# Prompt mixers: VectorE puts the level masks on the product as it leaves PSUM

## The chip, the cores and the metric

One core of one Trainium2 chip runs the whole step in one launch. The time is device microseconds of that core, the median of several executions. The profile is one execution, recorded by the hardware profiler; its times are counted from the start of its span.

## What is computed

One layer of a hybrid decoder over 2048 prompt tokens and 64 sample tokens: an input projection, three kinds of recurrent mixers (mLSTM, gated DeltaNet, HGRN2), an output projection and a squared-ReLU feed-forward. The change lies in the gated-DeltaNet part of the prompt mixers. For each of 6 heads and each chunk of tokens it needs the solution of a unit lower triangular system:

```python
lmat = where(strict, einsum('bhtk,bhsk->bhts', kb, kh) * exp(where(strict, diff, 0.0)), 0.0)
rhs = concatenate([vh * bh[..., None], kb * exp(g)[..., None]], axis=-1)
sol = triangular_solve(eye + lmat, rhs, left_side=True, lower=True, unit_diagonal=True)
```

## The kernel before

The stages run one after another: prologue, input projection, gates, prompt mixers, sample mixers, output projection, feed-forward. The prompt mixers (`prompt_mixers`) take 16 tiles of 128 tokens. Within each tile, all 6 heads are handled side by side in tiles of 128 x 6 x 128 elements (768 columns).

The inverse of identity plus L is built up by halving, in `LEVELS` = 7 levels. Level 0 handles pairs, level 1 groups of four, and so on. `lt` is the transposed matrix L (L2295, from PSUM `pa` and the decays `bd`). `x` is the inverse so far and `xt` its transpose; at each level only the off-diagonal corners of the level's blocks are new. A level is a ring over the engines:

- TensorE, `level_product(l)` (L1948): the level's part of -L times `x`, into `pa` or `pb`.
- ScalarE, `copy(l)` (L2060): that product from PSUM into `m1`.
- TensorE, `level_update(l)` (L1963): first `onto`, which puts `x` into PSUM through an identity matrix, then six products with `m1` on top of it (released by `m1_copy`), then six products of `m1` with `xt`, the change of the transpose.
- ScalarE, `inverse(l)` (L2070): the new `x` from PSUM. VectorE, `update(l)` (L2271): adds the change to `xt` (L2282).

In levels 0 to 4 (below `BLOCKY` = 5) the level's part of L is a masked and negated copy `cl[l % 3]`, which GpSimd makes (L2182), five products of 768 columns per tile, from `lt` and the mask `level`. Levels 5 and 6 use one negated copy `ltr` of the whole of `lt`, made by ScalarE (L2093) for every tile already, and take only the corners out of PSUM (L2067, L2277, L2287).

The order of the work is written out by hand, engine by engine, and engines meet through counted semaphores. The groups between the levels are the rest of the tile before: on TensorE `state_queries`, `mlstm`, `solved`, `hgrn`, `outputs`, `states`, `finish`. On VectorE they are the normalisation of the mLSTM (`den`, L2311 to L2313), the next tile's decays (L2238 `mix_cc`, L2240 `mix_dc`, L2243 `mix_ex`) between levels 1 and 2, `y`, `hs` and `hq` (L2321 to L2336) between 2 and 3, and `gs`, `cm` and the sum of squares `ss` (L2343 to L2351) between 3 and 4. On GpSimd the `cl` products are followed by `hk` (L2188, L2190), which waits for `e` and for TensorE's `hgrn` group (semaphore `ho`), then, after VectorE's `hq`, by the differences of the next tile (L2164, L2159) and its `bd` (L2149, L2151). VectorE's scaling of `y` by the head norms is L2359.

Of the kernel before, what the change touches and what calls it, by code (L numbers as in the profile page):

```python
# [8 lines left out]
F32 = mybir.dt.float32  # L9
F32R = mybir.dt.float32r  # L10
ALU = mybir.AluOpType
ACT = mybir.ActivationFunctionType
AX = mybir.AxisListType

P = 128
# [7 lines left out]
MH, GH, HH = 6, 6, 4  # L23
# [833 lines left out]
LEVELS = P.bit_length() - 1  # L857
HEADS_BY_PAIR = [0, 3, 1, 4, 2, 5]
BLOCKY = 5
# [818 lines left out]
def prompt_mixers(nc, d, keep):  # L1678

    with ExitStack() as ctx:  # L1680
# [8 lines left out]
        late = sb("late", [P, 2, P])  # L1689
        bd = sb("bd", [P, MH, P])  # L1690
        pm, at_, lt, xf, wn = (sb(n, [P, MH, P]) for n in ("pm", "attn", "lt", "xf", "wn"))
        cl = sb("cl", [P, 3, MH, P], F32R)
        x, xt, m1 = (sb(n, [P, MH + 1, P], F32R) for n in ("x", "xt", "m1"))
        ltr = sb("ltr", [P, MH, P], F32R)
        blocky = {l: sb(f"m1_{l}", [P, MH + 1, P], F32R) for l in range(BLOCKY, LEVELS)}
# [18 lines left out]
        pa, pb, pc, pd = bank("pa"), bank("pb"), bank("pc"), bank("pd")  # L1714
        za_in, zb_in, zg_in, rb_in, y_out = ([S(f"{n}{u}") for u in range(2)] for n in ("za_in", "zb_in", "zg_in", "rb_in", "y_out"))
        picked = [S(f"picked{par}") for par in range(2)]
        CONSTS = 2
        const_n = 64
        W = HD + 1
        U = 2 * (LEVELS - 1)  # L1720
# [96 lines left out]
        @block.tensor  # L1817
        def _(pe):
            pe.wait_ge(S("const_in"), const_n)
            pe.wait_ge(S("consts"), CONSTS)  # L1820

            def body(t, u, r, first=False, last=False, tail=False):
# [123 lines left out]
                    mm.then_inc(S("round"), 1)  # L1946

                def level_product(l):  # L1948
                    if l < BLOCKY:
                        pe.wait_ge(S("cl"), v(BLOCKY, l + 1))  # L1950
                    else:
                        pe.wait_ge(S("ltr"), v(1, 1))
                    lhs = lambda h: cl[:, l % 3, h, :] if l < BLOCKY else ltr[:, h, :]
                    if l:
                        pe.wait_ge(S("x"), v(LEVELS, l))
                        six(product_in(l), lhs, lambda h: pair_of(x, h), "m1")
                        return
                    if not first:
                        pe.wait_ge(S("xf"), b(1, 1))
                    onto(pb, ident_r[:, 0, :], lambda par: ident_r[:])  # L1960
                    add(pb, lhs, lambda h: ident_r[:, 2:4, :], "m1")
# [73 lines left out]
        def _(act):  # L2035
# [20 lines left out]
            def body(t, u, r, first=False, last=False, tail=False):  # L2056
                v = lambda n, c: t * n + c
                b = lambda n, c: t * n + c - n

                def copy(l):  # L2060
                    act.wait_ge(S("m1"), v(LEVELS, l + 1))
                    src = pv(product_in(l), P)
                    if l < BLOCKY:
                        act.activation(hm(m1[:, 0:MH]), src, ACT.Copy).then_inc(S("m1_copy"), 1)
                        return
                    for rows, cols in corners(l):
                        ins = act.activation(hm(m1_of(l)[rows, 0:MH, cols]), src[rows, :, :, cols], ACT.Copy)  # L2067
                    ins.then_inc(S("m1_copy"), 1)
# [70 lines left out]
        @block.gpsimd  # L2139
        def _(pool):  # L2140
            pool.memset(zero[:], 0.0).then_inc(S("zero"), 1)
            pool.wait_ge(S("zero"), 1)
            pool.wait_ge(S("const_in"), const_n)
            pool.wait_ge(S("consts"), CONSTS)

            def decays(t, u):

                pool.wait_ge(S("ex"), t + 1)
                pool.tensor_tensor(bd[:], ex[u][:, :, 1, :], rb[u][:, :, 2, :], ALU.mult).then_inc(S("bd"), 1)  # L2149
                pool.wait_ge(S("bd"), t * 2 + 1)  # L2150
                pool.tensor_tensor(bd[:], bd[:], late[:, 1:2, :].broadcast_to([P, MH, P]), ALU.mult).then_inc(S("bd"), 1)  # L2151

            def differences(t, u, r):

                g = zb[u][:, B_HG0:NBR:2, :]
                pool.wait_ge(zb_in[u], 32 * (r + 1))
                for l in range(LEVELS + 2):
                    if l == LEVELS:
                        ins = pool.tensor_tensor(e[:, l], g, zero[:].unsqueeze(2).broadcast_to([P, 2, P]), ALU.add)  # L2159
                        continue  # L2160
                    size, at = (2 << l, (1 << l) - 1) if l < LEVELS else (P, P - 1)
                    gv = g.rearrange("p j (n b) -> p j n b", b=size)
                    for j in range(2):
                        ins = pool.tensor_tensor(e[:, l, j].rearrange("p (n b) -> p n b", b=size), gv[:, j],  # L2164
                                                 gv[:, j, :, at:at + 1].broadcast_to([P, P // size, size]), ALU.subtract)
                ins.then_inc(S("diff"), 1)

            differences(0, 0, 0)
            decays(0, 0)

            def body(t, u, r, first=False, last=False, tail=False):
                v = lambda n, c: t * n + c
                b = lambda n, c: t * n + c - n
                if tail:
                    return
                pool.wait_ge(S("lt"), v(1, 1))
                for l in range(BLOCKY):
                    if l >= 3:
                        pool.wait_ge(S("m1"), v(LEVELS, l - 2))
                    if l == 3:  # L2180
                        pool.wait_ge(S("xt"), v(LEVELS, 1))
                    pool.tensor_tensor(cl[:, l % 3], lt[:], level[:, l + 1:l + 2, :].broadcast_to([P, MH, P]), ALU.mult  # L2182
                                       ).then_inc(S("cl"), 1)
                kr = zb[u][:, B_HG0 + 1:NBR:2, :]
                pool.wait_ge(S("e"), v(1, 1))
                if not first:
                    pool.wait_ge(S("ho"), b(1, 1))
                pool.tensor_tensor(hk[:, 0:LEVELS], e[:, 0:LEVELS], kr.unsqueeze(1).broadcast_to([P, LEVELS, 2, P]),  # L2188
                                   ALU.mult).then_inc(S("hk"), 1)
                pool.tensor_tensor(hk[:, LEVELS], e[:, LEVELS + 1], kr, ALU.mult).then_inc(S("hk"), 1)  # L2190
                if not last:
                    pool.wait_ge(S("hq"), v(1, 1))
                    pool.wait_ge(S("hk"), v(2, 2))
                    differences(t + 1, 1 - u, r + u)
                    decays(t + 1, 1 - u)
            tiles(body)

        @block.vector
        def _(dve):
# [15 lines left out]
                dve.memset(tile[:].bitcast(F32), 0.0)  # L2215
            dve.tensor_scalar(ident_r[:, 3, :], keep["ident"][:], 0.0, None, ALU.mult)
            dve.tensor_scalar(ident_2[:], keep["ident"][:], 2.0, None, ALU.mult)
            dve.tensor_copy(ident_r[:, 0:3, :], keep["ident"][:].unsqueeze(1).broadcast_to([P, 3, P])).then_inc(S("level_read"), 1)
            dve.wait_ge(S("level_read"), 1)
            dve.tensor_scalar(level[:], level[:], -1.0, None, ALU.mult).then_inc(S("consts"), 1)  # L2220
            ident4 = keep["ident"][:].unsqueeze(1).unsqueeze(1).broadcast_to([P, 2, 3, P])
            dve.wait_ge(S("consts"), CONSTS)
            STEPS = 32
# [24 lines left out]
            def body(t, u, r, first=False, last=False, tail=False):  # L2248
# [20 lines left out]
                                ins.then_inc(S("masked"), 1)  # L2269

                def update(l):  # L2271
                    if l >= BLOCKY:
                        dve.wait_ge(S("u"), v(U, 2 * l - 1))
                        dve.wait_ge(S("x"), v(LEVELS, l))
# [29 lines left out]
                    then(dve.tensor_tensor(hm(num[:]), pv(pd, W, 3 * W), colh(o, Q_WI, W), ALU.mult))  # L2304
                    dve.tensor_tensor(hm(num[:]), hm(num[:]), pv(pd, W), ALU.add).then_inc(S("num"), 1)
                if not tail:
                    dve.wait_ge(S("cl"), v(BLOCKY, 1))
                    dve.tensor_tensor(hm(xt[:, 0:MH]), ident4, hm(cl[:, 0].bitcast(F32)), ALU.add).then_inc(S("xt"), 1)
                if not first:
                    dve.wait_ge(S("num"), b(1, 1))  # L2310
                    then(dve.scalar_tensor_tensor(den[:, 0, :], num[:, :, HD], -1.0, num[:, :, HD], ALU.mult, ALU.max))  # L2311
# [756 lines left out]
```

## Time and profile before

| | us |
|---|---|
| median of 3 runs | 3625.7 (3625.65 to 3627.26) |
| profiled execution, its own time | 3626.71 |
| its span | 3624.9 |

| engine | busy us | share of the span |
|---|---|---|
| TensorE | 3286.9 | 91% |
| VectorE | 1829.1 | 50% |
| ScalarE | 1414.2 | 39% |
| GpSimd | 430.5 | 12% |

Shares over the whole span mix stages with different limits: GpSimd works in the mixers alone. The prompt mixers lie between about 980 and 1720 us. A timeline gives an instruction's start and duration on its engine; an entry with xN covers N instructions of one line. What stands in brackets is the idle time of the engine before it and what ended it. Durations of consecutive instructions overlap slightly. In the page the granted clock of TensorE over the span is 0.951 of full.

### The profile page before, as it was taken

What the parts mean: (1) busy time and instruction counts of PE and PEld (TensorE: products, weight loads), DVE (VectorE), ACT (ScalarE), POOL (GpSimd) and SP (SyncE); (2) the same over time, 40 slices, a digit from 0 to 9 for tenths busy, and PEclk for the clock granted to TensorE, in tenths of its full rate; (3) what the DMA queues carried; (4) which work ended last, traced back from release to release, by engine and by line L of the source; (5) the groups of instructions that cost most, each with busy time, mean ns of one, the idle gap of its engine ahead of it and who ended that gap; (6) DMA issues with size and microseconds to landing.
All of it is one profiled execution on the core that took longest, in us unless ns stands there. A gap on an engine that the chain in (4) does not pass through costs nothing. (4 is left out here: it accounts for less than half of the span.)

```text
span 3624.9 us, 52375 instructions
## 1 busy us (share of the span) xinstructions
PE 3286.9 (91%) x21605; PEld 2986.4 (82%) x21605; DVE 1829.1 (50%) x2931; ACT 1414.2 (39%) x2100; POOL 430.5 (12%) x442
## 2 busy tenths in 40 slices
PE   4899999998289899898569889999999999999998
PEld 3799999998278888787548679999999999999987
DVE  6232333221278888886457634454454454454465
ACT  6333422322145455553035433343343343333454
POOL 0000000000166565552200000000000000000000
PEclk6999999999599999998679989999999999999999
DMA  5222323221722222221246473344354344343353
GB/s 195 50 60 66 72 72 83 84 68 54 263 77 88 88 94 96 88 76 39 76 142 219 182 254 133 127 175 150 118 191 151 127 164 152 133 160 142 134 206 115
DMA packets 232385, 449.98 MB, mean 124 GB/s; under 512 B 41382, under 2 KB 115292, under 8 KB 228028
## 3 DMA queue, kind: packets, MB, share of 16 engines
q1 hardware_dynamic: 230020, 428.07, 34.9%
q10 hardware_dynamic: 2128, 18.56, 1.4%
q8 instruction: 172, 2.82, 0.3%
q14 instruction: 65, 0.53, 0.0%
HBM read 363.11 MB, written 83.47 MB: 123 GB/s over the span
## 5 line engine op out<-in xcount | busy, mean ns | idle before, releaser
L2779 PE MATMUL ff_p<-ff_h_hi,ff_w_hi 128*128 128x384 f32 (+1 forms) x1536 | 502.9, 327 | 24.9 <-DMA ff_h_lo<-tmp_h 24.9
L2781 PE MATMUL ff_p<-ff_h_hi,ff_w_lo 128*128 128x384 f32 (+1 forms) x1536 | 503.1, 328 | 0.0
L2780 PE MATMUL ff_p<-ff_h_lo,ff_w_hi 128*128 128x384 f32 (+1 forms) x1536 | 502.3, 327 | 0.0
L412 PE MATMUL pin_pz<-hi,pin_whi 128*128 128x424 f32 (+1 forms) x1320 | 469.0, 355 | 14.2 <-DVE pin_wlo L528 14.2
L413 PE MATMUL pin_pz<-lo,pin_whi 128*128 128x424 f32 (+1 forms) x1320 | 466.7, 354 | 0.0
L414 PE MATMUL pin_pz<-hi,pin_wlo 128*128 128x424 f32 (+1 forms) x1320 | 466.6, 353 | 0.0
L2798 PE MATMUL ff_p<-ff_w_lo,ff_f_hi 128*128 128x512 f32 (+1 forms) x1088 | 426.7, 392 | 0.0
L2799 PE MATMUL ff_p<-ff_w_hi,ff_f_lo 128*128 128x512 f32 (+1 forms) x1088 | 426.5, 392 | 0.0
L2797 PE MATMUL ff_p<-ff_w_hi,ff_f_hi 128*128 128x512 f32 (+1 forms) x1088 | 423.8, 389 | 0.0
L2882 DVE TENSOR_TENSOR ff_w_lo<-ff_w,ff_w_hi 128x1024 fp32r<-128x1024 f32 x192 | 235.1, 1224 | 346.4 <-ACT ff_w_hi L2830 346.4
L2830 ACT ACTIVATE ff_w_hi<-ff_w 128x1024 fp32r<-128x1024 f32 x192 | 203.6, 1060 | 389.0 <-PE ff_p L2799 384.6
L2779 PEld LDWEIGHTS ff_p<-ff_h_hi,ff_w_hi 128*128 128x128 f32 x1536 | 290.2, 189 | 34.0 <-DMA ff_h_lo<-tmp_h 25.0
L447 ACT ACTIVATE pin_z<-pin_pz,cols 128x424 f32<-128x424 f32 (+1 forms) x165 | 114.4, 702 | 515.5 <-PE pin_pz L414 416.8
L2780 PEld LDWEIGHTS ff_p<-ff_h_lo,ff_w_hi 128*128 128x128 f32 x1536 | 290.1, 189 | 7.3
L2838 ACT ACTIVATE ff_relu<-ff_p 128x384 f32<-128x384 f32 (+1 forms) x192 | 90.9, 473 | 515.4 <-PE ff_p L2781 515.4
L2781 PEld LDWEIGHTS ff_p<-ff_h_hi,ff_w_lo 128*128 128x128 f32 x1536 | 290.0, 189 | 0.0
L2890 DVE TENSOR_TENSOR ff_sq<-ff_relu 128x384 f32<-128x384 f32 (+1 forms) x192 | 102.7, 535 | 364.5 <-ACT ff_relu L2838 364.5
L528 DVE TENSOR_TENSOR pin_wlo<-pin_w,pin_whi 128x1024 fp32r<-128x1024 f32 x33 | 40.4, 1225 | 479.4 <-ACT pin_whi L440 479.4
L2877 DVE TENSOR_TENSOR ff_w_lo<-ff_w,ff_w_hi 128x1024 fp32r<-128x1024 f32 x192 | 235.0, 1224 | 83.0 <-ACT ff_w_hi L2823 66.2
L412 PEld LDWEIGHTS pin_pz<-hi,pin_whi 128*128 128x128 f32 x1320 | 248.6, 188 | 19.4 <-issue 15.3
L413 PEld LDWEIGHTS pin_pz<-lo,pin_whi 128*128 128x128 f32 x1320 | 248.8, 188 | 5.1 <-issue 1.0
L414 PEld LDWEIGHTS pin_pz<-hi,pin_wlo 128*128 128x128 f32 x1320 | 248.8, 188 | 4.2
(522 smaller groups left out, 5526.2 us busy)
## 6 DMA issues: line engine op xcount, KB each, us to landing
ff_w<-in_w_unit SPq DMA_DIRECT2D x192, 512.0 KB, 5.2
ff_w<-in_w_unit SPq DMA_DIRECT2D x48, 2048.0 KB, 8.0
tmp_z<-pin_z SPq DMA_DIRECT2D x32, 1024.0 KB, 5.2
mix_rb<-tmp_rows_p SPq DMA_DIRECT2D x16, 1152.0 KB, 5.7
pin_w<-in_w_in SPq DMA_DIRECT2D x33, 512.0 KB, 5.0
gat_wa<-in_w_ada ACTq DMA_DIRECT2D x8, 2048.0 KB, 28.3
mix_zb<-tmp_z SPq DMA_DIRECT2D x16, 640.0 KB, 4.2
tmp_h<-op_h_hi SPq DMA_DIRECT2D x17, 512.0 KB
```

The lines of the kernel that those rows point to most:

```text
L412: pe.matmul(pz[:, g, 0:n], whi[:, u, k], hi[:, k, at:at + n], start=(k == 0), stop=False)
L413: pe.matmul(pz[:, g, 0:n], whi[:, u, k], lo[:, k, at:at + n], start=False, stop=False)
L414: mm = pe.matmul(pz[:, g, 0:n], wlo[:, u, k], hi[:, k, at:at + n], start=False, stop=(k == KT - 1))
L2779: pe.matmul(dst, w1_hi[:, u, k], hi, start=(k == 0), stop=False)
L2780: pe.matmul(dst, w1_hi[:, u, k], lo, start=False, stop=False)
L2781: mm = pe.matmul(dst, w1_lo[:, u, k], hi, start=False, stop=(k == KT - 1))
L2797: pe.matmul(dst, f_hi[:, u, cols], w2_hi[:, u, ocs, :], start=(j == 0), stop=False)
L2798: pe.matmul(dst, f_hi[:, u, cols], w2_lo[:, u, ocs, :], start=False, stop=False)
L2799: mm = pe.matmul(dst, f_lo[:, u, cols], w2_hi[:, u, ocs, :], start=False, stop=(j == J - 1))
L2830: act.activation(w2_hi[:, c % 2], w2[:, four % 2, :, c % 4, :], ACT.Copy).then_inc(w2_hi_ready, 1)
L2877: dve.tensor_tensor(w1_lo[:, c % 2], w1[:, c % 4], w1_hi[:, c % 2].bitcast(F32), ALU.subtract).then_inc(w1_lo_ready, 1)
L2882: dve.tensor_tensor(w2_lo[:, c % 2], w2[:, (c // 4) % 2, :, c % 4, :], w2_hi[:, c % 2].bitcast(F32), ALU.subtract).then_inc(w2_lo_ready, 1)
```

## The change

The level masks move from the operand to the result. GpSimd makes one `cl`, for level 0, from the negated mask `level_n`. Levels 1 to 4 multiply with `ltr`, the whole negated matrix, and VectorE multiplies the product by the level's mask as it takes it out of PSUM into `m1` (in `update(l)`, ahead of its wait for TensorE's second group). The masks for this stand transposed in `level_t`; TensorE transposes them once at the start and VectorE copies them from PSUM. ScalarE's copies of levels 1 to 4 go, and `level` is no longer negated as a whole.

```diff
@@ -1689,7 +1689,9 @@
         late = sb("late", [P, 2, P])
         bd = sb("bd", [P, MH, P])
         pm, at_, lt, xf, wn = (sb(n, [P, MH, P]) for n in ("pm", "attn", "lt", "xf", "wn"))
-        cl = sb("cl", [P, 3, MH, P], F32R)
+        cl = sb("cl", [P, MH, P], F32R)
+        level_n = sb("level_n", [P, P])
+        level_t = sb("level_t", [P, BLOCKY - 1, P])
         x, xt, m1 = (sb(n, [P, MH + 1, P], F32R) for n in ("x", "xt", "m1"))
         ltr = sb("ltr", [P, MH, P], F32R)
         blocky = {l: sb(f"m1_{l}", [P, MH + 1, P], F32R) for l in range(BLOCKY, LEVELS)}
@@ -1714,7 +1716,7 @@
         pa, pb, pc, pd = bank("pa"), bank("pb"), bank("pc"), bank("pd")
         za_in, zb_in, zg_in, rb_in, y_out = ([S(f"{n}{u}") for u in range(2)] for n in ("za_in", "zb_in", "zg_in", "rb_in", "y_out"))
         picked = [S(f"picked{par}") for par in range(2)]
-        CONSTS = 2
+        CONSTS = 3
         const_n = 64
         W = HD + 1
         U = 2 * (LEVELS - 1)
@@ -1817,6 +1819,9 @@
         @block.tensor
         def _(pe):
             pe.wait_ge(S("const_in"), const_n)
+            for l in range(1, BLOCKY):
+                mm = pe.transpose(pa[:, 0, (l - 1) * P:l * P], level[:, l + 1, :], keep["ident"][:])
+            mm.then_inc(S("masks"), 1)
             pe.wait_ge(S("consts"), CONSTS)
 
             def body(t, u, r, first=False, last=False, tail=False):
@@ -1946,11 +1951,11 @@
                     mm.then_inc(S("round"), 1)
 
                 def level_product(l):
-                    if l < BLOCKY:
-                        pe.wait_ge(S("cl"), v(BLOCKY, l + 1))
+                    if l == 0:
+                        pe.wait_ge(S("cl"), v(1, 1))
                     else:
                         pe.wait_ge(S("ltr"), v(1, 1))
-                    lhs = lambda h: cl[:, l % 3, h, :] if l < BLOCKY else ltr[:, h, :]
+                    lhs = lambda h: ltr[:, h, :] if l else cl[:, h, :]
                     if l:
                         pe.wait_ge(S("x"), v(LEVELS, l))
                         six(product_in(l), lhs, lambda h: pair_of(x, h), "m1")
@@ -2058,11 +2063,10 @@
                 b = lambda n, c: t * n + c - n
 
                 def copy(l):
+                    if l < BLOCKY:
+                        return
                     act.wait_ge(S("m1"), v(LEVELS, l + 1))
                     src = pv(product_in(l), P)
-                    if l < BLOCKY:
-                        act.activation(hm(m1[:, 0:MH]), src, ACT.Copy).then_inc(S("m1_copy"), 1)
-                        return
                     for rows, cols in corners(l):
                         ins = act.activation(hm(m1_of(l)[rows, 0:MH, cols]), src[rows, :, :, cols], ACT.Copy)
                     ins.then_inc(S("m1_copy"), 1)
@@ -2174,13 +2178,7 @@
                 if tail:
                     return
                 pool.wait_ge(S("lt"), v(1, 1))
-                for l in range(BLOCKY):
-                    if l >= 3:
-                        pool.wait_ge(S("m1"), v(LEVELS, l - 2))
-                    if l == 3:
-                        pool.wait_ge(S("xt"), v(LEVELS, 1))
-                    pool.tensor_tensor(cl[:, l % 3], lt[:], level[:, l + 1:l + 2, :].broadcast_to([P, MH, P]), ALU.mult
-                                       ).then_inc(S("cl"), 1)
+                pool.tensor_tensor(cl[:], lt[:], level_n[:].unsqueeze(1).broadcast_to([P, MH, P]), ALU.mult).then_inc(S("cl"), 1)
                 kr = zb[u][:, B_HG0 + 1:NBR:2, :]
                 pool.wait_ge(S("e"), v(1, 1))
                 if not first:
@@ -2215,9 +2213,10 @@
                 dve.memset(tile[:].bitcast(F32), 0.0)
             dve.tensor_scalar(ident_r[:, 3, :], keep["ident"][:], 0.0, None, ALU.mult)
             dve.tensor_scalar(ident_2[:], keep["ident"][:], 2.0, None, ALU.mult)
-            dve.tensor_copy(ident_r[:, 0:3, :], keep["ident"][:].unsqueeze(1).broadcast_to([P, 3, P])).then_inc(S("level_read"), 1)
-            dve.wait_ge(S("level_read"), 1)
-            dve.tensor_scalar(level[:], level[:], -1.0, None, ALU.mult).then_inc(S("consts"), 1)
+            dve.wait_ge(S("masks"), 1)
+            dve.tensor_copy(level_t[:], pa[:, 0, :].rearrange("p (l c) -> p l c", c=P)).then_inc(S("consts"), 1)
+            dve.tensor_scalar(level_n[:], level[:, 1, :], -1.0, None, ALU.mult)
+            dve.tensor_copy(ident_r[:, 0:3, :], keep["ident"][:].unsqueeze(1).broadcast_to([P, 3, P])).then_inc(S("consts"), 1)
             ident4 = keep["ident"][:].unsqueeze(1).unsqueeze(1).broadcast_to([P, 2, 3, P])
             dve.wait_ge(S("consts"), CONSTS)
             STEPS = 32
@@ -2269,6 +2268,10 @@
                                 ins.then_inc(S("masked"), 1)
 
                 def update(l):
+                    if l < BLOCKY:
+                        dve.wait_ge(S("m1"), v(LEVELS, l + 1))
+                        dve.tensor_tensor(hm(m1[:, 0:MH]), pv(product_in(l), P), level_t[:, l - 1, :].unsqueeze(1).unsqueeze(1)
+                                          .broadcast_to([P, 2, 3, P]), ALU.mult).then_inc(S("m1_copy"), 1)
                     if l >= BLOCKY:
                         dve.wait_ge(S("u"), v(U, 2 * l - 1))
                         dve.wait_ge(S("x"), v(LEVELS, l))
@@ -2304,8 +2307,8 @@
                     then(dve.tensor_tensor(hm(num[:]), pv(pd, W, 3 * W), colh(o, Q_WI, W), ALU.mult))
                     dve.tensor_tensor(hm(num[:]), hm(num[:]), pv(pd, W), ALU.add).then_inc(S("num"), 1)
                 if not tail:
-                    dve.wait_ge(S("cl"), v(BLOCKY, 1))
-                    dve.tensor_tensor(hm(xt[:, 0:MH]), ident4, hm(cl[:, 0].bitcast(F32)), ALU.add).then_inc(S("xt"), 1)
+                    dve.wait_ge(S("cl"), v(1, 1))
+                    dve.tensor_tensor(hm(xt[:, 0:MH]), ident4, hm(cl[:].bitcast(F32)), ALU.add).then_inc(S("xt"), 1)
                 if not first:
                     dve.wait_ge(S("num"), b(1, 1))
                     then(dve.scalar_tensor_tensor(den[:, 0, :], num[:, :, HD], -1.0, num[:, :, HD], ALU.mult, ALU.max))
```

The VectorE queue of a tile in the middle, around levels 1 and 2. `mix_m` is `m1`; `mix_pa` and `mix_pb` are PSUM. Before:

```order
L2313 RECIPROCAL mix_den<-mix_den 128x6
L2282 TENSOR_TENSOR mix_xt<-mix_xt,mix_pa 128x768
L2238 TENSOR_SCALAR mix_cc<-cols_p 128x48
L2240 TENSOR_SCALAR mix_dc<-mix_dec 64x6 x2
L2243 TENSOR_TENSOR mix_ex<-mix_rb,mix_late 128x1536
L2282 TENSOR_TENSOR mix_xt<-mix_xt,mix_pb 128x768
```

And now:

```order
L2316 RECIPROCAL mix_den<-mix_den 128x6
L2273 TENSOR_TENSOR mix_m<-mix_pa,mix_level_t 128x768
L2285 TENSOR_TENSOR mix_xt<-mix_xt,mix_pa 128x768
L2237 TENSOR_SCALAR mix_cc<-cols_p 128x48
L2239 TENSOR_SCALAR mix_dc<-mix_dec 64x6 x2
L2242 TENSOR_TENSOR mix_ex<-mix_rb,mix_late 128x1536
L2273 TENSOR_TENSOR mix_m<-mix_pb,mix_level_t 128x768
L2285 TENSOR_TENSOR mix_xt<-mix_xt,mix_pb 128x768
```

The mask products of levels 1 and 2 stand ahead of the `xt` of their level; the second stands behind the three lines of the decays.

The same queue around levels 3 and 4. Before:

```order
L2336 TENSOR_TENSOR mix_hq<-mix_e,mix_zb 128x2048
L2282 TENSOR_TENSOR mix_xt<-mix_xt,mix_pa 128x768
L2343 SCALAR_TENSOR_TENSOR mix_gs<-mix_gs,mix_dc,mix_pc 128x64 x3
L2347 SCALAR_TENSOR_TENSOR mix_cm<-mix_cm,mix_dc,mix_pc 128x65 x3
L2351 TENSOR_REDUCE mix_ss<-mix_sq 128x16
L2282 TENSOR_TENSOR mix_xt<-mix_xt,mix_pb 128x768
```

And now:

```order
L2339 TENSOR_TENSOR mix_hq<-mix_e,mix_zb 128x2048
L2273 TENSOR_TENSOR mix_m<-mix_pa,mix_level_t 128x768
L2285 TENSOR_TENSOR mix_xt<-mix_xt,mix_pa 128x768
L2346 SCALAR_TENSOR_TENSOR mix_gs<-mix_gs,mix_dc,mix_pc 128x64 x3
L2350 SCALAR_TENSOR_TENSOR mix_cm<-mix_cm,mix_dc,mix_pc 128x65 x3
L2354 TENSOR_REDUCE mix_ss<-mix_sq 128x16
L2273 TENSOR_TENSOR mix_m<-mix_pb,mix_level_t 128x768
L2285 TENSOR_TENSOR mix_xt<-mix_xt,mix_pb 128x768
```

The masks of levels 3 and 4 stand behind `hq` and behind the sum `ss`.

The ScalarE queue around level 1 (`vn` from the `solved` group, then `kd`). Before:

```order
L2089 ACTIVATE mix_vn<-mix_pc 128x384
L2064 ACTIVATE mix_m<-mix_pa 128x768
L2093 ACTIVATE mix_ltr<-mix_lt 128x768
L2096 ACTIVATE mix_y<-mix_pd 128x2x2x64
L2097 ACTIVATE mix_kd<-mix_pd 128x256
L2072 ACTIVATE mix_x<-mix_pb 128x768
L2064 ACTIVATE mix_m<-mix_pb 128x768
L2072 ACTIVATE mix_x<-mix_pa 128x768
```

And now:

```order
L2093 ACTIVATE mix_vn<-mix_pc 128x384
L2097 ACTIVATE mix_ltr<-mix_lt 128x768
L2100 ACTIVATE mix_y<-mix_pd 128x2x2x64
L2101 ACTIVATE mix_kd<-mix_pd 128x256
L2076 ACTIVATE mix_x<-mix_pb 128x768
L2076 ACTIVATE mix_x<-mix_pa 128x768
```

The copies to `m1` are gone, and `ltr` directly follows `vn`.

## Rows read from the trace of the kernel before

**Rows 1.** Stretches: busy us (instructions) per engine, granted clock, DMA share, GB/s.

```profile
1432.60:1476.00 43.40, 39.71 (x458) 35.53 (x454) 36.23 (x79) 22.92 (x41) 25.34 (x26) 1.00 0.27 92
...
1476.00:1523.30 47.30, 41.20 (x456) 36.76 (x454) 39.20 (x78) 22.92 (x41) 25.23 (x26) 0.96 0.25 84
```

**Rows 2.** Timeline, VectorE: start us, duration us, engine, line; `mix_lt` of five tiles.

```profile
1210.56 0.95 DVE L2295 TENSOR_TENSOR mix_lt<-mix_pa,mix_bd 128x768 f32<-128x768 f32 x1
...
1259.13 0.95 DVE L2295 TENSOR_TENSOR mix_lt<-mix_pa,mix_bd 128x768 f32<-128x768 f32 x1
...
1432.61 0.95 DVE L2295 TENSOR_TENSOR mix_lt<-mix_pa,mix_bd 128x768 f32<-128x768 f32 x1
...
1475.97 0.95 DVE L2295 TENSOR_TENSOR mix_lt<-mix_pa,mix_bd 128x768 f32<-128x768 f32 x1
...
1523.31 0.95 DVE L2295 TENSOR_TENSOR mix_lt<-mix_pa,mix_bd 128x768 f32<-128x768 f32 x1
```

**Rows 3.** Timeline, VectorE and TensorE: scaling of `y` in two tiles, TensorE's wait.

```profile
1459.58 1.34 DVE L2359 TENSOR_TENSOR mix_y<-mix_y,mix_ss 128x1024 f32<-128x1024 f32 x1
...
1502.93 4.42 DVE L2359 TENSOR_TENSOR mix_y<-mix_y,mix_ss 128x1024 f32<-128x1024 f32 x1
...
1508.25 0.95 PE L1841 MATMUL mix_pb<-mix_x,mix_ltr 128*128 128x256 f32 x6 [2.61 <-DVE mix_x L2277]
```

**Rows 4.** Timeline of the steady tile, level 1; [idle before <-releaser] in brackets.

```profile
1433.64 9.71 POOL L2182 TENSOR_TENSOR mix_cl<-mix_lt,mix_level 128x768 fp32r<-128x768 f32 x5 [11.25 <-DVE mix_lt L2295]
...
1437.14 0.79 ACT L2072 ACTIVATE mix_x<-mix_pb 128x768 fp32r<-128x768 f32 x1
...
1438.08 0.95 PE L1841 MATMUL mix_pa<-mix_x,mix_cl 128*128 128x256 f32 x6
...
1438.69 0.49 ACT L2089 ACTIVATE mix_vn<-mix_pc 128x384 f32<-128x384 f32 x1
...
1439.08 0.81 ACT L2064 ACTIVATE mix_m<-mix_pa 128x768 fp32r<-128x768 f32 x1
...
1439.90 0.84 ACT L2093 ACTIVATE mix_ltr<-mix_lt 128x768 fp32r<-128x768 f32 x1
...
1440.89 0.70 PE L1923 MATMUL mix_pb<-mix_x,mix_ident_r 128*128 128x512 f32 x2
...
1443.11 0.95 DVE L2282 TENSOR_TENSOR mix_xt<-mix_xt,mix_pa 128x768 fp32r<-128x768 f32 x1 [1.31 <-PE mix_pa L1841]
```

**Rows 5.** Timeline of the steady tile, level 2.

```profile
1443.32 4.01 POOL L2188 TENSOR_TENSOR mix_hk<-mix_e,mix_zb 128x1792 f32<-128x1792 f32 x1
...
1443.98 3.40 DVE L2238 TENSOR_SCALAR mix_cc<-cols_p 128x48 f32<-128x48 f32 x1
...
1446.42 0.86 PE L1929 MATMUL mix_pa<-mix_m,mix_xt 128*128 128x256 f32 x6
...
1447.13 0.87 PE L1841 MATMUL mix_pb<-mix_xt,mix_m 128*128 128x256 f32 x6
...
1448.27 1.76 DVE L2243 TENSOR_TENSOR mix_ex<-mix_rb,mix_late 128x1536 f32<-128x1536 f32 x1
...
1449.94 0.95 DVE L2282 TENSOR_TENSOR mix_xt<-mix_xt,mix_pb 128x768 fp32r<-128x768 f32 x1
```

**Rows 6.** Timeline of the steady tile, levels 3 and 4.

```profile
1451.51 0.97 PE L1929 MATMUL mix_pb<-mix_m,mix_xt 128*128 128x256 f32 x6
...
1452.32 0.88 PE L1841 MATMUL mix_pa<-mix_xt,mix_m 128*128 128x256 f32 x6
...
1452.38 2.28 DVE L2336 TENSOR_TENSOR mix_hq<-mix_e,mix_zb 128x2048 f32<-128x2048 f32 x1
...
1454.59 0.94 DVE L2282 TENSOR_TENSOR mix_xt<-mix_xt,mix_pa 128x768 fp32r<-128x768 f32 x1
...
1456.16 0.87 PE L1929 MATMUL mix_pa<-mix_m,mix_xt 128*128 128x256 f32 x6
...
1457.78 0.95 DVE L2282 TENSOR_TENSOR mix_xt<-mix_xt,mix_pb 128x768 fp32r<-128x768 f32 x1
```

## The prediction

> **What bounds the kernel now.** I read the page first: TensorE is busy 91% of the span, and the change touches only the prompt mixers, where 16 tiles of 128 tokens pass one after another. Then the stretches by engine: a steady tile keeps TensorE busy 39.7 of 43.4 us at the full granted clock, VectorE 36.2, ScalarE 22.9, GpSimd 25.3 [rows 1]. So TensorE bounds the tile, VectorE is second, ScalarE has half its time free. What the change takes away (ScalarE, GpSimd) was spare; what it adds goes to the engine with least room beside TensorE.
>
> Third, the length of a tile, from one `mix_lt` to the next: 1432.61 to 1475.97 is 43.36 us. Two of the 16 are longer: the one from 1210.56 to 1259.13 (48.57) and the one from 1475.97 to 1523.31 (47.34) [rows 2]. In the second the row-wise scaling of `y` (L2359) took 4.42 us instead of 1.34, and TensorE waited 2.61 us behind it for `x` [rows 3]; in the first it is the same picture. Together they cost 5.20 + 3.97 = 9.2 us over the steady tile. The `y` instruction accounts for 3.1 us of each; the other 2.1 and 0.9 are TensorE at half speed (1.2 of 2.4 GHz) after its wait: the granted clock of the second is 0.96, that of the steady tile 1.00 [rows 1].
>
> Last, the timeline of the steady tile, level by level. Each level is a ring: product (TensorE), copy of the product to `m1`, update (TensorE), copy of `x` (ScalarE), next product. TensorE fills the copy's time with a group of the tile before, so the copy of 0.8 us is hidden.
>
> **The change part by part.** I write times on the clock of the steady tile and let the delay D grow.
>
> Level 1, the negated matrix `ltr`. Product 1 used `cl`, there since long, and started 0.15 us after `x` (1437.14 + 0.79 = 1437.93) at 1438.08. Now it needs `ltr`, whose copy stands on ScalarE behind the near copies and `vn`. The `m1` copy ahead of it goes, so `ltr` starts where that one did, 1439.08, and ends 0.84 later at 1439.92; product 1 follows at 1440.07. **D = 1.99** [rows 4]. The mask itself (0.95 us, as `mix_lt`, also a product of PSUM and an SBUF matrix [rows 2], against 0.81 for ScalarE's copy [rows 4]) ends near 1442.0. TensorE's own fill, from product 1 to the update, is 2.81 us (1438.08 to 1440.89) and ends later, at 1442.88. So the mask costs nothing here; without that fill it would cost 1.1.
>
> Level 2. VectorE's order now is: `xt` of level 1, then the next tile's decays (L2238, L2240, L2243), then mask 2. ScalarE had copied `m1` with nothing ahead of it. The decays end at a time that GpSimd sets: `mix_cc`, a copy of 48 columns, took 3.40 us because it sat until the first `hk` (1443.32 + 4.01 = 1447.33) was done [rows 5]. Does `hk` now start earlier, with four of the five `cl` products gone (9.71 us for five [rows 4], 1.9 each)? No: it also waits for TensorE's group behind product 1, which ended near 1441.1 and now ends D later, at 1443.1. So `hk` stays where it was, `mix_ex` still ends near 1449.94, and mask 2 runs 1449.94 to 1450.89. The update's masked half starts 0.14 later at 1451.03, where before it was at 1446.42: **D = 4.61** [rows 5].
>
> The Trainium skill (SBUF — State Buffer, Who interferes with whom) says that a VectorE instruction with two SBUF inputs, or in a two-port mode, is fully blocked by a GpSimd instruction that holds the shared port. The 3.40 us of `mix_cc` agree. By it, fewer GpSimd products are a gain for VectorE's small instructions ahead of level 1; by the rows it is none, since VectorE then waits 1.31 us for TensorE before `xt` [rows 4]. If the port alone set the end there, the sum would be 15 x 1.3 = 20 us lower than mine.
>
> Level 3. `xt` of level 2 waited for the decays before (1449.94) and now waits for TensorE's second half, 1447.13 + 0.87 + 4.61 = 1452.61, so it starts at 1452.72. From there to the end of `hq` is 4.72 us as before (1454.66 less 1449.94), since the same instructions stand between. `hq` ends at 1457.44, mask 3 runs 1457.37 to 1458.32 (consecutive instructions overlap by 0.07, as 1454.59 shows), the update gets its matrix at 1458.46 against 1451.51: **D = 6.95** [rows 6].
>
> Level 4. `xt` of level 3 now waits for TensorE, 1452.32 + 0.88 + 6.95 = 1460.15, start 1460.25. The state updates and the sum `ss` stand behind it; from there to the next level's instruction it was 3.19 us (1454.59 to 1457.78). Mask 4 runs 1463.44 to 1464.39, the update gets it at 1464.53 against 1456.16: **D = 8.37** [rows 6]. Levels 5 and 6 are untouched, and behind them TensorE and VectorE are near full, so nothing is made up.
>
> Sum: 15 tiles x 8.37 = +125.6. The first tile has none of the fills on VectorE except decays and `hq`; I take +4, an estimate of half a tile's loss, with 0 and 8.4 as ends. The constants (four transposes, a 512-column copy for a scaling of 1024 columns) come to +0.3, an estimate, ends -1 and +2. The collision of `y` should go: `hq` ends at 1457.44, GpSimd's differences after it took some 7 us before, so they end near 1464.5, while `y` moves by D to 1467.95 [rows 3, 6]. That returns the 9.2 us; ends 0 and -9.2. Subtotal **+120.7**.
>
> **The clock.** New waits of TensorE per tile, each the time above less my estimate of the end of the fill before it: about 1.8 us before product 1, 2.5 at level 2, 2.9 at level 3, 1.8 at level 4. The two waits of 2.6 us in the trace were each followed by half clock, worth 2.13 and 0.9 us, mean 1.5. With two waits per tile of that size, not each of which need bring the fall, I take 1.4 falls per tile: 2.1 x 15 = **+31.5**. Below, the bound is 0; above, TensorE stays at half clock through the levels: a group of six products of 256 columns takes 0.95 at full clock, about 0.7 more at half, and eight such groups stand in the ring from product 1 to update 4: 5.6 per tile, +84.
>
> Total +152 on the profiled span of 3624.9, that is 3777. The profiled run itself took 3626.7, the median is 3625.7, so the forecast is **3778**.
>
> The Trainium skill (VectorE: DVE Perf Modes, Specifications) says that VectorE sits closer to SBUF and ScalarE closer to PSUM, which speaks against moving a PSUM read to VectorE. The rows agree, 0.95 against 0.81 us. On its own that is 4 x 0.14 x 16 = 9 us at most, an estimate from those rows; what costs here is the place in the queue.
>
> **The rivals.**
> (a) The clock stays full, the masks wait as above: 3625.7 + 121 = 3747. For it: the waits are cut by short groups; against: both waits of 2.6 us in the trace were followed by the fall [rows 1, 3].
> (b) The clock stays at half through the levels: 3625.7 + 121 + 84 = 3831.
> (c) The masks are hidden and only `ltr` costs: 15 x 1.99 + 1 - 9.2 = +22, 3647. It needs VectorE to reach masks 2 to 4 before TensorE does; the order of its queue and the 3.40 us of `mix_cc` speak against it.
> (d) The other side, faster: the freed GpSimd time unblocks VectorE and removes the collision, and TensorE waits for neither `ltr` nor masks. The place is L2359, the price 9.2 us: 3616.5, -0.25%. It decides only if `ltr` is ready before product 1's old start, 1438.08; but `vn`, ahead of it on the same engine, starts only at 1438.69 [rows 4]. Nothing in the trace speaks for it except those two long tiles.
> (e) A wash: losses at levels 2 to 4 a tenth of mine, against the 9.2 us.
>
> **How the numbers follow.** Chances: forecast 0.60, (a) 0.16, (b) 0.12, (c) 0.08, (d) 0.02, (e) 0.02. The range takes in the forecast with the bounds of its small terms and all of (a), down to 3738 (the first tile, the constants at their low ends and a little less wait), and up to 3822, most of the way to (b); what is left out is (c), (d), (e) and the upper half of (b), 0.18. A measurement of this kernel tells about 0.2%, 7 us, from no change. Faster by more is (d), 0.02; within it (e), 0.02; slower the rest, 0.96.
>
> **What would show it.** Per tile 50 to 54 us between two `mix_lt`. Product 1 waits for ScalarE's `ltr`, about 2 us later than before. TensorE waits for VectorE's `m1` at levels 2, 3 and 4, not at 1, by about 2.5, 2.9 and 1.8 us. `mix_cc` still takes over a microsecond behind `hk`, less than 3.4. `y` takes 1.2 to 1.4 us in every tile. The granted clock over a tile is between 0.8 and 0.97. ScalarE falls by some 3.2 us a tile and GpSimd by 7.7, neither of which shows in the time. Wrong it would be if `hk` started right behind the one `cl` product, since then the decays end some 4 us sooner and level 2 costs only D of level 1, or if the clock holds at 1.00.

## The result and the profile after

The changed kernel takes 3784.2 us (median of 4, 3777.8 to 3792.8); the kernel before, run beside it, 3626.5. The ratio is 1.0441, with a 95% interval of 1.0421 to 1.0461: slower by 4.4%. The profiled execution took 3784.08 us, its span is 3782.3.

The page's first and second part, where they answer the table of before (busy us, share, instructions; then the granted clock in 40 slices, of the changed kernel and of the kernel before):

```profile
PE 3361.5 (89%) x21609; PEld 3050.5 (81%) x21609; DVE 1782.6 (47%) x2996; ACT 1363.3 (36%) x2036; POOL 296.0 (8%) x378
...
PEclk6999999998688888998768989999999999999999
```

```profile
PEclk6999999999599999998679989999999999999999
```

ScalarE and GpSimd have lost the work that was taken away, VectorE is busy less as well (1782.6 against 1829.1), and the kernel is slower. The difference lies in the mixers, which begin in the eleventh slice: from the twelfth to the sixteenth the granted clock shows 8 where it showed 9.

Stretches of one tile each, columns as in [rows 1]: the tile of the changed kernel with least half clock, and one that is typical.

```profile
1536.38:1588.07 51.69, 41.70 (x458) 36.73 (x455) 34.17 (x83) 19.70 (x37) 16.80 (x22) 0.97 0.24 78
1208.26:1263.37 55.11, 45.47 (x458) 40.63 (x454) 32.70 (x83) 19.70 (x37) 16.79 (x22) 0.88 0.23 72
```

VectorE's timeline, from one `mix_lt` (L2298 now) to the next, to hold against [rows 2]:

```profile
1208.26 0.95 DVE L2298 TENSOR_TENSOR mix_lt<-mix_pa,mix_bd 128x768 f32<-128x768 f32 x1
1263.37 0.95 DVE L2298 TENSOR_TENSOR mix_lt<-mix_pa,mix_bd 128x768 f32<-128x768 f32 x1
...
1536.38 0.95 DVE L2298 TENSOR_TENSOR mix_lt<-mix_pa,mix_bd 128x768 f32<-128x768 f32 x1
1588.07 0.95 DVE L2298 TENSOR_TENSOR mix_lt<-mix_pa,mix_bd 128x768 f32<-128x768 f32 x1
```

The steady tile of 43.36 us has become 51.69 us where the clock is nearly whole (0.97), 55.11 us where it is 0.88. The mean of the 14 tiles from the second `mix_lt` (1044.10) to the last (1802.41) is 54.17. I call the first of these the clean tile; the next rows are from its timeline. Level 1, against [rows 4]:

```profile
1542.46 0.49 ACT L2093 ACTIVATE mix_vn<-mix_pc 128x384 f32<-128x384 f32 x1
1542.97 0.84 ACT L2097 ACTIVATE mix_ltr<-mix_lt 128x768 fp32r<-128x768 f32 x1
...
1543.87 0.98 PE L1846 MATMUL mix_pa<-mix_x,mix_ltr 128*128 128x256 f32 x6 [1.86 <-ACT mix_ltr L2097]
...
1544.95 0.96 DVE L2273 TENSOR_TENSOR mix_m<-mix_pa,mix_level_t 128x768 fp32r<-128x768 f32 x1 [3.11 <-PE mix_pa L1846]
...
1546.68 0.70 PE L1928 MATMUL mix_pb<-mix_x,mix_ident_r 128*128 128x512 f32 x2
...
1547.08 4.04 POOL L2186 TENSOR_TENSOR mix_hk<-mix_e,mix_zb 128x1792 f32<-128x1792 f32 x1 [7.84 <-PE mix_pd L1891]
```

TensorE waited 1.86 us for `ltr`. The mask is done long before TensorE comes back to the level at 1546.68. `hk` waits for TensorE and starts 10.70 us into the tile, as before (10.71). It does so in two of the 14 tiles; in the others TensorE is at half clock for some or all of level 1, and `hk` starts 11.2 to 13.2 us into the tile. Levels 2, then 3 and 4, against [rows 5] and [rows 6]:

```profile
1549.72 1.45 DVE L2237 TENSOR_SCALAR mix_cc<-cols_p 128x48 f32<-128x48 f32 x1
...
1552.05 1.76 DVE L2242 TENSOR_TENSOR mix_ex<-mix_rb,mix_late 128x1536 f32<-128x1536 f32 x1
1553.72 0.95 DVE L2273 TENSOR_TENSOR mix_m<-mix_pb,mix_level_t 128x768 fp32r<-128x768 f32 x1
...
1554.73 0.98 PE L1934 MATMUL mix_pa<-mix_m,mix_xt 128*128 128x256 f32 x6 [2.35 <-DVE mix_m L2273]
...
1558.91 2.29 DVE L2339 TENSOR_TENSOR mix_hq<-mix_e,mix_zb 128x2048 f32<-128x2048 f32 x1
1561.11 0.95 DVE L2273 TENSOR_TENSOR mix_m<-mix_pa,mix_level_t 128x768 fp32r<-128x768 f32 x1
...
1562.12 0.98 PE L1934 MATMUL mix_pb<-mix_m,mix_xt 128*128 128x256 f32 x6 [2.79 <-DVE mix_m L2273]
...
1564.09 1.62 PE L1846 MATMUL mix_pb<-mix_x,mix_ltr 128*128 128x256 f32 x6 [0.15 <-ACT mix_x L2076]
...
1566.00 1.21 DVE L2354 TENSOR_REDUCE mix_ss<-mix_sq 128x16 f32<-128x1024 f32 x1
...
1567.13 0.95 DVE L2273 TENSOR_TENSOR mix_m<-mix_pb,mix_level_t 128x768 fp32r<-128x768 f32 x1
...
1568.13 0.98 PE L1934 MATMUL mix_pa<-mix_m,mix_xt 128*128 128x256 f32 x6 [0.64 <-DVE mix_m L2273]
```

At each of the three levels the mask starts as the instruction ahead of it on VectorE ends (`mix_ex`, `hq`, the sum `ss`), and TensorE's update follows 0.06 us behind the mask's end. Over 13 tiles of the changed kernel, TensorE's waits (us in total, times, longest):

```profile
PE mix_pa L1934 <- DVE mix_m L2273: 37.4, 26, 2.3
PE mix_pb L1934 <- DVE mix_m L2273: 35.6, 13, 2.8
PE mix_pa L1846 <- ACT mix_ltr L2097: 22.5, 13, 1.9
```

None of the three was there before. The first row holds levels 2 and 4 together, the second is level 3. In the tiles other than the clean one part of the waits is taken up by slower matmuls: level 2's is 1.3 us on the mean of the 13. TensorE in the tile from 1099.19, at level 1 and at level 3:

```profile
1106.67 1.65 PE L1846 MATMUL mix_pa<-mix_x,mix_ltr 128*128 128x256 f32 x6 [1.86 <-ACT mix_ltr L2097]
...
1127.21 1.65 PE L1934 MATMUL mix_pb<-mix_m,mix_xt 128*128 128x256 f32 x6 [2.79 <-DVE mix_m L2273]
...
1128.66 1.48 PE L1846 MATMUL mix_pa<-mix_xt,mix_m 128*128 128x256 f32 x6
```

Six products of 256 columns take 1.65 and 1.48 us instead of 0.95 and 0.88 [rows 4, 6]: that is the half clock, 1.2 GHz, behind the waits of 1.86 and 2.79 us.

### The profile page after: what moved, and what is told of

It reads as the page before. It is cut to its first block and busy times, and to the rows that moved or that the text cites. A ratio compares the mean times of both kernels' runs of the same rounds, so it can differ in the third digit from the quotient of the medians.

```text
span 3782.3 us, 52319 instructions
## 1 busy us (share of the span) xinstructions
PE 3361.5 (89%) x21609; PEld 3050.5 (81%) x21609; DVE 1782.6 (47%) x2996; ACT 1363.3 (36%) x2036; POOL 296.0 (8%) x378
```

## The experiments

All are run beside the kernel before, whose median was 3624, 3620 and 3625 us in the three groups of runs, so ratios compare best. Tile lengths are means of 14 tiles of each run's profile, from the second `mix_lt` to the last. The theory: a mask costs what its place in VectorE's queue makes it late, `ltr` what its place on ScalarE does, and the waits are dear beyond their length because TensorE's clock falls behind them. The rivals: VectorE's added load, the work taken from GpSimd, or one bottleneck that hides the rest.

**GpSimd makes `ltr`.** 

```diff
-                    act.activation(ltr[:], lt[:], ACT.Copy, scale=-1.0).then_inc(S("ltr"), 1)
+                pool.tensor_tensor(ltr[:], lt[:], minus[:].unsqueeze(1).broadcast_to([P, MH, P]), ALU.mult).then_inc(S("ltr"), 1)
```

> The changed kernel, but GpSimd makes ltr right behind its one cl product (a product with a tile of -1), and ScalarE's ltr copy goes. Theory (each place in a queue has its own price): product 1 no longer waits for ScalarE, so its 2.0 us go; hk and with it the decays come 2.0 us sooner, so levels 2 to 4 keep their own losses of 2.5, 2.3 and 1.4 us and the tile loses 6.3 instead of 8.3 us: 15 x 2.0 = 30 us less than 3784, and up to 25 us more if the clock no longer falls before product 1, so 3729 to 3754. Rival (the end of the decays on VectorE sets level 2 whatever came before, the wait for ltr lies in its shadow): within 8 us of 3784.

Measured 3736.0 us, ratio 1.0306 (1.0281 to 1.0330); the tile is 51.16 us, 3.0 less. TensorE's waits over 12 tiles:

```profile
PE mix_pa L1935 <- DVE mix_m L2274: 44.5, 24, 2.3
PE mix_pb L1935 <- DVE mix_m L2274: 30.4, 12, 3.1
```

No wait for `ltr` is left. Those for the masks stayed: 6.2 us a tile where the changed kernel had 5.6, since fewer slow matmuls take up part of them (level 2's is 2.2 to 2.3 us in every tile). The wait for `ltr` cost its 2.0 us, not in the shadow of level 2: in a tile of 49.72 us with the clean tile's granted clock (0.97) the update of level 2 is 16.3 us into the tile instead of 18.35. The other 1.0 us a tile goes with the clock, 0.941 over the span against 0.932; by this run alone that is argued, not shown.

**The decays behind level 2.**

```diff
-                if not last:
-                    decays(t + 1, 1 - u, r + u, then)
                 if not tail:
                     update(2)
+                if not last:
+                    decays(t + 1, 1 - u, r + u, then)
```

> The changed kernel, but VectorE does the next tile's decays behind xt of level 2, not ahead of mask 2. Theory (VectorE's queue from xt of level 2 to mask 3 is what sets the end, so the decays only change places): level 2's update comes 2.5 us sooner, mask 3 then stands behind decays (some 2.6 us with nothing blocking them) and the fills and hq, so level 3 gives it back: 3776 to 3792. Rival (each wait counts for itself, so 2.5 us a tile are saved): 3784 - 38 = 3746, less still if the clock falls less often.

Measured 3804.9 us, ratio 1.0492 (1.0466 to 1.0517). VectorE's timeline in one tile, and TensorE's waits over 11:

```profile
1283.52 0.95 DVE L2273 TENSOR_TENSOR mix_m<-mix_pb,mix_level_t 128x768 fp32r<-128x768 f32 x1
...
1288.13 0.18 DVE L2237 TENSOR_SCALAR mix_cc<-cols_p 128x48 f32<-128x48 f32 x1
...
1294.06 0.95 DVE L2273 TENSOR_TENSOR mix_m<-mix_pa,mix_level_t 128x768 fp32r<-128x768 f32 x1
```

```profile
PE mix_pb L1934 <- DVE mix_m L2273: 54.3, 11, 4.9
...
PE mix_pa L1934 <- DVE mix_m L2273: 16.2, 11, 1.9
```

Mask 2 (1283.52) no longer waits for the decays, and the wait at level 2 is gone (the remaining 16.2 us in `mix_pa` are level 4's). Mask 3 (1294.06) now stands behind them, and level 3's wait has grown from 2.8 to 4.9 us. Not one microsecond of the 2.5 was saved: the stall moved one level on. It got slower, by 1.0 us a tile, outside what I had expected. The waits of levels 2 to 4 together are 6.4 us a tile here, against 5.6 in the changed kernel: level 2 lost its mean of 1.3 us, level 3 gained 2.2 and level 4 stayed near 1.5. The granted clock over the span is lower too (0.926 against 0.932). What each of the two costs was not told apart.

**The masks first.** The same instructions, in another order on VectorE:

```diff
                 if not tail:
+                    level_mask(1)
                     update(1)
+                    level_mask(2)
                 if not last:
                     decays(t + 1, 1 - u, r + u, then)
                 if not tail:
                     update(2)
+                    level_mask(3)
...
                     update(3)
+                    level_mask(4)
```

> The changed kernel, but each mask stands at the first place in VectorE's queue where its product can be ready: mask 2 ahead of the decays, mask 3 directly behind xt of level 2, mask 4 directly behind xt of level 3. The same instructions, other order. Theory (the masks cost by what stands ahead of them, not by what they take): only the 2.0 us of ltr and some 0.9 us (masks 3 and 4 behind an xt of 0.95) stay, 15 x 2.9 = 44 us over the kernel before, less 9 for the lost collisions of y: 3650 to 3675. Rival (the price is VectorE's added work, 3.8 us a tile, or the clock, wherever it stands): above 3700.

Measured 3690.5 us, ratio 1.0186 (1.0156 to 1.0216): 94 us of the 158 gone, by order alone. It is 15 us over the range I gave. Two neighbouring stretches of this run, and TensorE's waits over 12 tiles:

```profile
1376.20:1421.70 45.50, 40.01 (x452) 35.54 (x452) 33.52 (x82) 19.84 (x39) 17.31 (x22) 1.00 0.29 88
1421.70:1469.80 48.10, 42.83 (x452) 38.32 (x452) 32.97 (x82) 19.89 (x39) 17.31 (x22) 0.93 0.26 85
```

```profile
PE mix_pa L1846 <- ACT mix_ltr L2097: 22.2, 12, 1.9
...
PE mix_pa L1928 <- DVE mix_xt L2286: 8.3, 12, 0.7
```

One tile, at full clock, took 45.5 us, with the same wait of 1.86 us for `ltr`; nearly all others 48.0 at 0.93. The masks' waits are gone. What is left is `ltr`, 1.9 us, and I had left out what that wait does to the clock: 2.5 us a tile, more than the wait itself.

**Both.** `ltr` by GpSimd and the masks first.

> Both: ltr made by GpSimd and the masks at the first possible places. Theory: no wait for ltr, 0.9 us a tile of late masks, less the two collisions: 3625 to 3645. Rival (VectorE is now the bound of the tile and its work of 4 masks at 0.95 us shows in full): 3665 or more.

Measured 3626.4 us, ratio 1.0011 (0.9994 to 1.0029): as fast as the kernel before, with all four masks on VectorE. Thirteen of the 14 tiles take 43.5 us. One took 49.6, at a granted clock of 0.86: half clock set in as that tile began, though TensorE had waited no longer than 0.8 us at a time since the tile before began. So a long wait is not the only occasion of half clock; what brought it there is open. In one of the thirteen:

```profile
1492.58 0.96 DVE L2273 TENSOR_TENSOR mix_m<-mix_pb,mix_level_t 128x768 fp32r<-128x768 f32 x1 [0.28 <-PE mix_pb L1847]
1493.46 0.19 DVE L2238 TENSOR_SCALAR mix_cc<-cols_p 128x48 f32<-128x48 f32 x1
...
1497.57 0.96 DVE L2273 TENSOR_TENSOR mix_m<-mix_pa,mix_level_t 128x768 fp32r<-128x768 f32 x1 [0.28 <-PE mix_pa L1847]
...
1503.09 0.95 DVE L2273 TENSOR_TENSOR mix_m<-mix_pb,mix_level_t 128x768 fp32r<-128x768 f32 x1
```

Masks 2 and 3 start as their products end (VectorE waits 0.28 us for them), and mask 4 directly follows `xt`. `mix_cc` takes 0.19 us, since `hk`, now 2.0 us sooner, ends within 0.2 us of its start. VectorE's added work does not show in the time. The scaling of `y` takes 1.8 us in 14 of its 16 tiles here and never 4, so its collision is short but not gone.

**Filling the wait for `ltr`.** The masks first, and ahead of product 1 twelve matmuls of 256 columns (identity by identity):

```diff
                     solved()
+                    if not tail:
+                        keep_busy(pc[:, 1, 0:2 * P], 12)
```

> e3_masks_first with twelve matmuls of 256 columns that nothing uses, put ahead of product 1 where TensorE waits 1.9 us for ltr; they take about 1.7 us there. No wait is taken away, work is added. Theory (of e3's 48.0 us a tile, 2.5 are half clock that follows this wait, as its one tile at full clock took 45.5): the clock stays whole and the tile takes 45.5: 3690 - 14 x 2.5 = 3655, range 3648 to 3664. Rival (the 2.5 us come from VectorE's queue or GpSimd): 3688 to 3700.

Measured 3652.9 us, ratio 1.0092 (1.0079 to 1.0105). Every one of the 14 tiles takes 45.5 us, at the full clock:

```profile
1086.00:1131.50 45.50, 41.48 (x468) 36.94 (x468) 33.52 (x82) 19.84 (x37) 17.33 (x22) 1.00 0.26 88
```

```profile
PE mix_pa L1846 <- ACT mix_ltr L2103: 4.6, 12, 0.4
```

The wait has shrunk from 1.9 to 0.4 us because useless work stands in it; product 1 starts no sooner. That work made the kernel 38 us faster (by the ratios 34), 2.5 us a tile. This is the clock, measured by itself.

**Filling the waits of the changed kernel.** The same before product 1, and 14 and 18 such matmuls ahead of the wait for `m1` at levels 2 and 3.

> The changed kernel with the same unused matmuls in three of TensorE's four new waits: 12 ahead of product 1, 14 ahead of the update of level 2, 18 ahead of that of level 3 (1.7, 2.0 and 2.5 us). Theory (of the 54.2 us a tile, 51.7 are waits and work at full clock and 2.5 the half clock): 3784 - 15 x 2.2 = 3751, range 3742 to 3762. Rival (the clock falls anyway, or its half is hidden in the waits): 3780 or more.

Measured 3755.5 us, ratio 1.0373 (1.0360 to 1.0387); the tile is 51.99 us, ten of the 14, at a granted clock of 1.00, between 51.4 and 51.6; the other four are at 0.94 to 0.97. So of the 10.8 us that a tile lost against the steady 43.36, at least 2.2 are half clock, and 2.7 if these ten are the measure.

**GpSimd's products put back**, four of them per tile, into a tile that nothing reads:

```diff
+                for l in range(1, BLOCKY):
+                    if l >= 3:
+                        pool.wait_ge(S("extra"), v(4, l - 2))
+                    pool.tensor_tensor(extra[:, (l - 1) % 2], lt[:], level[:, l + 1:l + 2, :].broadcast_to([P, MH, P]), ALU.mult
+                                       ).then_inc(S("extra"), 1)
```

> The changed kernel, with GpSimd's four other masked products put back, into a tile that nothing reads: only GpSimd's load and its use of the port it shares are as before. Theory (hk waits for TensorE's group behind product 1 and starts 10.7 us into the tile either way, and VectorE's small instructions have spare time there): 3776 to 3792. Rival (taking GpSimd's products away has given VectorE time that counts, up to 1.3 us a tile): 3784 + 20 = 3804 or more.

Measured 3784.4 us, ratio 1.0449 (1.0434 to 1.0464), the number of the changed kernel. VectorE's timeline here:

```profile
1270.89 1.77 DVE L2320 SCALAR_TENSOR_TENSOR mix_den<-mix_num 128x6 f32<-128x6 f32 x1
1272.69 1.75 DVE L2321 TENSOR_SCALAR mix_den<-mix_den 128x6 f32<-128x6 f32 x1
1274.47 0.19 DVE L2322 RECIPROCAL mix_den<-mix_den 128x6 f32<-128x6 f32 x1
```

The first two, on 6 columns, take 0.16 and 0.17 us in the changed kernel and 1.8 us beside GpSimd's products. GpSimd does hold VectorE up, by 3.2 us a tile in these two, and it costs nothing: behind mask 1, which comes next, VectorE still waits for TensorE, 5.3 us in this tile and 2.3 at the least.

**One mask more, at two places**, level 4 as shown, and level 1 in the other kernel.

```diff
+                        if l == 4:
+                            if t:
+                                dve.wait_ge(S("step"), t * STEPS)
+                            dve.tensor_tensor(hm(extra[:]), pv(product_in(l), P), level_t[:, l - 1, :].unsqueeze(1).unsqueeze(1)
+                                              .broadcast_to([P, 2, 3, P]), ALU.mult)
```

> The changed kernel; at level 4 VectorE makes the mask product twice, the first time into a tile that nothing reads: 0.95 us more in front of the update of level 4. Theory (TensorE waits there for VectorE, so the place has no slack): 15 x 0.95 = 14 us more, 3784 + 14 = 3798, with some half clock more, 3792 to 3808. Rival (the loss is one of the engine's whole load or of latency elsewhere, the place does not matter): the same number as for level 1.

> The changed kernel; the same instruction once more, but at level 1, where TensorE is busy with a group of 2.8 us between product and update. Theory: hidden, 3776 to 3792. Rival (VectorE's load counts wherever it stands): 3798 or more, as at level 4.

At level 4 it measured 3805.2 us, ratio 1.0494 (1.0469 to 1.0519), 0.9 us a tile more than the changed kernel; at level 1 3785.9, ratio 1.0435 (1.0405 to 1.0466), nothing more. The same 0.95 us cost all or nothing by their place.

**A fill moved out of the way**, in the kernel with both remedies and in the kernel before: the mLSTM part of `y` right behind the reciprocal.

```diff
                     then(dve.reciprocal(den[:, 1, :], den[:, 0, :]))
+                    dve.tensor_tensor(ym(y[:, Y_M:Y_G, :]), hm(num[:])[:, :, :, 0:HD],
...
                 if not first:
-                    dve.tensor_tensor(ym(y[:, Y_M:Y_G, :]), hm(num[:])[:, :, :, 0:HD],
...
```

> e4_both with one fill moved on VectorE: the mLSTM part of y (0.55 us) from between mask 3 and hq to right behind the reciprocal, where VectorE waits 0.5 us for TensorE. Theory (in e4 TensorE waits 0.7 us for xt of level 3, which stands behind those fills): 0.45 us a tile less, 3626 - 7 = 3619, so the same as or a little faster than the kernel before. Rival (mask 1 or another wait takes it over): 3626 to 3630.

> The kernel before, with the mLSTM part of y moved on VectorE from between level 2 and hq to right behind the reciprocal, where it waits 1.3 us for TensorE. Theory (TensorE waits 0.7 us for xt of level 2 and 0.5 us for that of level 3, and the second stands behind that instruction): 0.4 to 0.5 us a tile less, 3614 to 3620 against 3620 to 3626, if the two collisions of y do not become more. Rival (GpSimd's five products now hold it up, or the collisions grow by one or two at 4 to 5 us each): 3620 to 3632.

The first measured 3620.2 us (12 runs, 3613.7 to 3630.1) against 3620.2 of the kernel before: ratio 0.9998 (0.9989 to 1.0008). Eleven of its 14 tiles take 43.0 us instead of 43.5, and TensorE's wait for `xt` has fallen from the first of these rows (the kernel with both, 12 tiles) to the second (13 tiles):

```profile
PE mix_pa L1929 <- DVE mix_xt L2287: 8.3, 12, 0.7
```

```profile
PE mix_pa L1929 <- DVE mix_xt L2287: 3.0, 13, 0.2
```

The second measured 3628.6, ratio 1.0000 (0.9985 to 1.0015), so the rival's number. Its undisturbed tiles are 43.06 us, 0.3 less, but three of them took 47 in its profile, where the kernel before had two long ones. The collisions of `y` are still there:

```profile
L2359 DVE TENSOR_TENSOR mix_y<-mix_y,mix_ss x16: 1218/1343/4265, 1067.1 to 1717.2; 128x1024 f32<-128x1024 f32 x16
```

(shortest, median and longest in ns.) Whether the third is due to the move or to chance, one profile can't tell. No version beat the kernel before by more than the measurement can tell.

## Why the prediction came out

The forecast was 3778 in 3738 to 3822; 3784 was measured. By its steps, against the clean tile:

- **`ltr`, D = 1.99.** Product 1 starts 7.49 us into the tile (1543.87 less 1536.38) instead of 5.47 [rows 2, 4]: 2.02. Confirmed alone by the kernel in which GpSimd makes `ltr`.
- **Level 2, D = 4.61.** The update's masked half is at 18.35 instead of 13.81 [rows 5]: 4.54. That `hk` would stay at its place and hold the decays was right, though `mix_cc` is held 1.45 us here and only some 0.6 us in most other tiles, where slower matmuls brought VectorE there later.
- **Level 3, D = 6.95.** 25.74 instead of 18.90: 6.84. **Level 4, D = 8.37.** 31.75 instead of 23.55 [rows 6]: 8.20. The tile: 51.69 less 43.36 = 8.33.
- **The clock, 2.1 us a tile.** 54.17 less 51.69 is 2.48. The mechanism is shown by the two kernels that fill the waits. What was mis-sized: I counted on waits of 2.5 us and more, but the wait of 1.9 us before product 1 is enough, as the kernel with the masks first showed. The four waits were put at 1.8, 2.5, 2.9 and 1.8 us; in the clean tile they are 1.86, 2.35, 2.79 and 0.64. Level 4's is short because half clock behind level 3's wait lies inside it: the product ahead of it takes 1.62 us instead of 0.96.
- **The picture as a whole** fits two tiles of 14. In the other twelve half clock around level 1 delays `hk`, `xt` and with them mask 2 (17.9 to 19.9 us into the tile instead of 17.3), so delay and clock mix there. That the delay stands by itself is seen in the kernel with filled waits, whose tiles at full clock take some 51.5 us, 8.1 over the steady tile, against a D of 8.37.
- **The first tile, +4**, was +5.7 (47.30 against 41.64 us from its `mix_lt` to the next); half clock lay over more of it (granted clock 0.78 against 0.85). **The constants, +0.3**: the first `mix_lt` comes at 996.80 instead of 995.57, +1.2. The kernel before with `y` moved, which has the old constants, has it at 998.75, so this difference shows nothing about them.
- **The collisions, -9.2.** `y` takes 1.2 us in all 16 tiles, against [rows 3]:

```profile
L2362 DVE TENSOR_TENSOR mix_y<-mix_y,mix_ss x16: 1212/1215/1224, 1082.8 to 1870.9; 128x1024 f32<-128x1024 f32 x16
```

On spans: 1.2 + 5.7 + 15 tiles. The 14 between the second and the last `mix_lt` took 758.3 us instead of 616.2, +142.1, collisions taken off; the last tile and what follows it, +8.4. Together 157.4, the difference of the two spans.

Of the rivals, (a), a whole clock, is refuted as a description of this run but met by the kernel with filled waits, 3755.5 against my 3747. (b), half clock through the levels, would be a tile of 57 us (51.69 + 5.6); the longest of the 14 is 55.2. (e), losses a tenth of mine, fell with the levels. (c), only `ltr` costs, became true when the masks went first, again with the clock added. (d) fell at the place I named: `ltr` isn't ready. That GpSimd's lighter load gives nothing back was argued in the prediction and is now shown.

## What to carry to other kernels

Before moving work to an engine with a low busy share, look at what stands ahead of it in that engine's queue at the moment it is needed: here 0.95 us instructions cost nothing or up to 2.5 us each, by place alone, and moving what stood ahead of one only moved the stall. The four masks could be had for nothing with two changes of order and owner; put a step that releases the bounding engine first, and fills behind it. A wait of TensorE costs its length and then the clock: price both, also for a wait under 2 us.

## What the runs showed that I had not expected

A wait of 1.9 us on TensorE in a tile otherwise busy was followed by half clock in 13 of the 14 tiles, and cost 2.5 us on top (48.0 against 45.5 us). Twelve useless matmuls in that wait took 38 us off the kernel. But one tile of 14 kept the full clock behind the same wait, and in the kernel with both remedies one tile fell to half clock, at a cost of 6 us, with no wait over 0.8 us ahead of it; why was not settled.
